# Mixture-of-experts phase: 28 light experts in place of 24, 25 units in place of 26

## What is computed

```python
scores = sigmoid(xf @ w_router)            # (264, 64)
...                                        # 4 of 8 groups, then the best 8 experts of them
gate = ...                                 # (264, 64), 0 for experts not chosen
h = silu(einsum('td,edf->tef', xb, w_gate)) * einsum('td,edf->tef', xb, w_up)
h = h * gb[..., None]
routed = einsum('tef,efd->td', h, w_down)  # 64 experts of 1024x256, 1024x256, 256x1024
shared = (silu(xf @ ws_gate) * (xf @ ws_up)) @ ws_down
```

## Time and profile before

| what | us |
|---|---|
| three runs, median (lowest to highest) | 1022.73 (1020.9 to 1023.9) |
| the profiled execution, its own time | 1022.15 |
| its span, first to last instruction | 1020.3 |
| mean granted TensorE clock | 0.974 |
| TensorE matmuls busy | 936.3 |
| VectorE, ScalarE, GpSimd busy | 504.5, 232.9, 244.0 |

### The profile page before, as it was taken

The page is one execution under the profiler, slowest core; times in us unless marked ns, Lnnn a source line. Parts: engine busy times, 40 slices in busy tenths (PEclk is TensorE's granted clock), DMA queues, the critical chain, the costliest instruction groups (busy, mean ns, idle before and its releaser), DMA issues.

```text
span 1020.3 us, 19336 instructions
## 1 busy us (share of the span) xinstructions
PE 936.3 (92%) x7882; PEld 555.5 (54%) x7882; DVE 504.5 (49%) x1040; ACT 232.9 (23%) x483; POOL 244.0 (24%) x281
## 2 busy tenths in 40 slices
PE   5999999999999998689999999999899799799795
PEld 4878877887787777536744334434333233233231
DVE  2148857885886596885523233333233223232234
ACT  3241134113411341344011111211111121111113
POOL 0039805950793099000100000000000000000000
PEclk9999999999999999979999999999899899899898
DMA  8643134114312407149589999999999999999961
GB/s 241 184 124 95 43 115 149 54 43 142 120 55 84 138 4 288 26 181 418 189 351 385 399 420 420 419 420 419 417 419 419 419 401 420 420 409 418 422 254 45
DMA packets 76742, 265.04 MB, mean 260 GB/s; under 512 B 12943, under 2 KB 44241, under 8 KB 51800
## 3 DMA queue, kind: packets, MB, share of 16 engines
q1 hardware_dynamic: 72791, 254.09, 64.4%
q0 software_dynamic: 3856, 9.64, 2.5%
HBM read 263.75 MB, written 5.89 MB: 264 GB/s over the span
## 4 chain that ended last, share of the span: by engine, by line
PE 67%; DMA 20%; DVE 6%; ACT 3%; SPq 2%; issue 2%; DVEq 0%; ACTq 0%
PE bank L1350 64%; DMA big<-in_w_up 17%; ACT big L1647 2%; SPq L401 2%; DMA big<-in_w_down 2%; DMA big<-in_w_in 1%; PE bank L629 1%; DVE big L1937 1%; PE bank L691 1%; ACT L1647 1%; DVE big L1994 1%; DVE big L1990 0%; PE bank L657 0%; DVE big L913 0%; DVE big L1185 0%
## 5 line engine op out<-in xcount | busy, mean ns | idle before, releaser
L1350 PE MATMUL bank<-big 64*64 64x64 f32 (+8 forms) x7412 | 878.6, 372 | 63.2 <-DMA big<-in_w_up 27.2
L1350 PEld LDWEIGHTS bank<-big 64*64 64x64 f32 (+4 forms) x7412 | 499.8, 143 | 401.7 <-issue 297.6
L1647 ACT ACTIVATE big<-bank 128x512 f32<-128x512 f32 (+8 forms) x283 | 121.9, 459 | 625.2 <-PE bank L1350 347.8
L1191 POOL DMA_INDIRECT big<-xg,big x26 | 26.3, 1010 | 501.2 <-PE bank L629 395.5
L2136 POOL TENSOR_SCALAR big<-big 128x256 f32<-128x256 f32 x120 | 127.3, 1062 | 0.4
L2148 POOL TENSOR_TENSOR big<-big 128x256 f32<-128x256 f32 x120 | 87.7, 730 | 0.3
L1099 DVE TENSOR_TENSOR big<-big,bank 128x512 f32<-128x512 f32 x104 | 71.5, 688 | 31.7 <-PE bank L1350 31.6
L1937 DVE SCALAR_TENSOR_TENSOR big<-big 128x256 f32<-128x256 f32 x120 | 74.4, 620 | 4.1
L1096 DVE TENSOR_TENSOR big<-big,bank 104x256 f32<-104x256 f32 x26 | 11.0, 422 | 118.9 <-issue 76.3
L1647 ACT ACTIVATE big<-big 128x272 f32<-128x272 f32 (+9 forms) x108 | 49.9, 505 | 42.3 <-DVE big L1872 11.3
L1061 DVE TENSOR_TENSOR big<-big,bank 128x256 f32<-128x256 f32 x26 | 11.0, 422 | 96.9 <-ACT big L1647 96.9
(11 more groups left out here) (156 smaller groups left out, 361.1 us busy)
## 6 DMA issues: line engine op xcount, KB each, us to landing
big<-in_w_gate SPq DMA_DIRECT2D x64, 1024.0 KB, 13.9
big<-in_w_up SPq DMA_DIRECT2D x64, 1024.0 KB, 17.3
big<-in_w_down SPq DMA_DIRECT2D x64, 1024.0 KB, 23.6
big<-in_w_in SPq DMA_DIRECT2D x29, 1024.0 KB, 5.4
big<-in_w_out SPq DMA_DIRECT2D x2, 2048.0 KB, 11.5
big<-in_state_wkv SPq DMA_DIRECT2D x32, 64.0 KB, 2.2
out_wkv_s<-big SPq DMA_DIRECT2D x32, 64.0 KB, 3.9
big<-in_x_prompt SPq DMA_DIRECT2D x2, 512.0 KB, 3.7
```

What stands on the lines that cost most here:

```text
L1191: pool.indirect_dma_start(out=x[0:n, :], out_offset=None, in_=xg, in_offset=bass.IndirectOffsetOnAxis(ap=idxu[0:n, col:col + 1], axis=0), ...
L1350: return nc.tensor.matmul(out_, lhsT=lhsT, rhs=rhs, start=start, stop=stop)
L1647: return nc.scalar.activation(out_, in_, f, **kw)
```

## The change

28 experts are light in place of 24. Fourteen triples and eleven pairs make 25 units; before there were twelve triples and fourteen pairs. Before, the order was PPP T and eleven times TP. Now it is PPP, six times TTP, and twice TP. With an odd number of units the last unit's output buffer is the other one (`ye[0]`, which is the third row of `x2p`), so the scratch row of the last Square and the buffer of the overflow pass move too.

```diff
-NSTATIC, NLIGHT = 6, 24
-UNITS = 'PPP' + 'T' + 'TP' * 11
+NSTATIC, NLIGHT = 6, 28
+UNITS = 'PPP' + 'TTP' * 6 + 'TP' * 2
...
-        xe1, ye1, oh1 = xe[0], ye[0], OH[0][:, :, 0:SLOTS]
+        xe1, ye1, oh1 = xe[0], ye[NU_E % 2], OH[0][:, :, 0:SLOTS]
...
-                link(fn(x2p[0:r, t, :], xrow[0:r, t, :], ACT.Square, accum_out=stat[0:r, t:t + 1]), 'act_chain')
+                link(fn(x2p[0:r, t % 2, :], xrow[0:r, t, :], ACT.Square, accum_out=stat[0:r, t:t + 1]), 'act_chain')
```

## The result

| what | before | after |
|---|---|---|
| median (lowest to highest), us | 1023.2 (1020.9 to 1023.9) | 1034.53 (1033.04 to 1035.69) |
| the profiled execution, its own time | 1022.15 | 1033.04 |
| its span | 1020.3 | 1031.2 |
| mean granted TensorE clock | 0.974 | 0.968 |

The ratio of after to before is 1.0105, with an interval of 1.0081 to 1.0128: slower by 11.3 us on the medians, 10.9 on the two profiled executions. The forecast was 6.2 us slower, 1028.4, with 1034.0 as the top of its range.

What follows compares the result with a forecast made beforehand. DMA bytes bound the edited stretch. Five idles +9.6, one gather -1.3 and the tail -2.1 make +6.2 on 1022.15, so 1028.4 us; range 1020.5 to 1034, chance of slower 0.64.

Steps and rivals of the forecast that it cites:

- The bound: In the stretch the change edits, weight bytes through the full DMA queue set the time: 39.9 us per triple and pair.
- The unit that is gone, at nothing: One unit of 26 removed, 17.6 us of TensorE work, gains nothing because the weight stream covers it.
- The rival in which it gives 17.6: TensorE as bound, the missing unit giving 17.6: 1004.6 us; chance 0.13 together with a weaker form, which holds nearly all.
- The gather, -1.3: One fewer gather call of token rows in the DMA queue, a gain of at most 1.3 us.
- The place and the mechanism: At five new triples behind triples, TensorE waits 5 to 9 us for up loads and the DMA queue then empties.
- e19: Expert, numbered in processing order; last of three in the first new triple behind a triple, up load landing at 632.5.
- The tail, -2.1: At the end, the last triple waits less than 1 us and its block takes a warm 7.9 us, gaining 2.1.
- The idle, 5 x 1.9 = 9.6: DMA queue idle behind five new triples that follow a triple, 1.9 us each, +9.6 in sum.
- 2.3 for the restart: A gate load into an empty queue takes 4.8 us to land, 2.3 more than its 2.49 of transfer.
- The waits for down loads: Near the end, TensorE waits 2.3 us for one down load, counted within the tail.
- upper bound of 2.9 per idle: Most that each queue idle was to cost: 5.3 us to land in place of 4.8, and 14.9 to the release.
- the u4 junction: The one triple behind a triple in the kernel before; its 0.9 us idle was taken as the lower bound.

Runs made afterwards that it cites:

- Run 2: Changed kernel, with combine(q-2) ahead of the first half of gate_up in each triple behind a triple: 1022.24 us, ratio 0.9989 to the kernel before.
- run 6: Changed kernel; combine, turn_hidden and down ahead of gate_up in triples from the seventh unit on, SyncE's down loads issued before its release wait: 1020.82 us, ratio 0.9979.
- run 7: Kernel before; combine, turn_hidden and down ahead of gate_up in triples from the seventh unit on, SyncE's down loads issued before its release wait: 1019.85 us, ratio 0.9968.
- run 11: Changed kernel, with only combine(q-2) ahead of gate_up's first half in triples from the seventh unit on and in the last pair: 1029.27 us, ratio 1.0054.

## Why the prediction was wrong, step by step

**The bound: right.** Bytes set the time from 585 us to the last triple. Runs 2, 6 and 7 differ in units, order and TensorE's waits, keep the queue full (DMA share 1.00 to 1.01), and lie within 3 us of each other.

**The unit that is gone, at nothing: right.** 15 us of TensorE work left the kernel and the time did not follow; runs 6 and 7 differ by 1 us, the kernel with fewer units being the slower. The rival in which it gives 17.6 falls.

**The gather, -1.3: right as a price.** Where nothing else is in the way, the landings of single loads across a gather are 1.25 us further apart in both traces, and after has one call fewer in the stretch. That this call gives its price back follows from the count; no run shows it by itself.

**The place and the mechanism: right.** u7 released its slots at 647.29 (647 forecast), the next gate load landed 4.8 later, at 652.1 (652 forecast). TensorE waits at u7, u10, u13, u16 and u19 4.0, 6.8, 7.2, 9.4 and 5.5 us, 32.8 in all where 5 to 9 each and some 30 were forecast. The wait of u7 is shorter than its forecast of 5.8 because u6 had waited 4.09 us for a down load (1.57 before) and released its slots at 622.40, 2.3 us later than before with the same instructions; e19's up load still landed at 632.57, before at 632.45. The share of the DMA engines falls below 1 at each of the five. The first blocks, 50 matmuls, ran at a clock of 0.72 to 0.85 (0.75 forecast); that of u7, then that of u23 behind its wait of 1.20:

```profile
632.70:642.90 10.20, 10.20 (x50) 3.34 (x51) 2.49 (x4) 0.00 (x0) 0.00 (x0) 0.77 1.02 425
...
975.16:983.06 7.90, 7.90 (x50) 3.00 (x51) 2.49 (x4) 0.00 (x0) 0.00 (x0) 1.00 1.02 424
```

**The tail, -2.1: right.** u23 waited 1.20 us, 0.2 more than the bound that was forecast, and its block took 7.90. From u23's start to the end of the span are 56.04 us, 58.10 before: -2.06.

**The idle, 5 x 1.9 = 9.6: the step that failed.** The mechanism was there at all five places, but each cost 2.5 us and not 1.9, 12.5 in all. This is 2.9 of the 4.6 us by which the profiled execution of after, 1033.04, lies above the forecast. Another 1.7 of queue time has no cause shown (below), and the median lies 1.5 over the profiled execution. The idle is in two pieces, and only the first was in my sum. The first is the time until the gate load of the release is in. From the landing of the second triple's up load to the release are 14.7, 13.9, 13.8, 14.7 and 15.3 us, 14.5 in the mean as forecast; with 2.3 for the restart and the 14.94 of queued loads off, the idles are 2.1, 1.3, 1.2, 2.1 and 2.7, together 9.3. So by my own measure the number was right. The Trainium skill, "DMA: Bandwidth & Descriptors", section "Anatomy of one DMA — SWDGE (gpsimd) path", gives some 2.0 us of fixed cost for a DMA of the GpSimd path. The trace has, for loads issued by SyncE, 2.3 to 2.4 over the 2.49 us of a full queue at the four restarts whose landing is on record, and the measurement decides.

The second piece is what comes after the first landing. I took the stream to be back in step as soon as the gate load is in. The up load lands behind it not 2.49 but 3.0, 3.7, 3.0 and 4.6 us later at the four places where both landings are on record. Counted from the last landing on record before each empty queue to the next gather, the landings lie 2.0, 1.7, 1.6, 3.6 and 3.6 us further apart than 2.485 a load and the usual 1.25 of the gather that starts there: 12.5 in all, 3.2 more than the 9.3 of the first piece. The first loads after an empty queue and that gather come together; which of the two slows the other, no run separated. Run 2 shows that it belongs to the empty queue: with the queue full, the gathers at the same places cost 1.25. A single place scatters, though. At u4, where the instructions are the same in both kernels, the same count gives 0.4 in before (583.25 to 602.25, seven loads) and 1.5 in after (580.23 to 602.82, eight loads). So the sum of five is firmer than any one of them.

The total can be read from the last triple's up load. The chain of after from 880 us:

```profile
887.42 10.12 DMA big<-in_w_up
...
917.33 17.40 DMA big<-in_w_down
...
955.38 19.64 DMA big<-in_w_up
```

It lands at 955.38 + 19.64 = 975.02, where before it was at 962.07: 12.95 later with one gather fewer, so 14.2 us of queue are lost. 12.5 of them are the junctions; the other 1.7 have no cause shown. The same count from e19's up load to this one, 124 loads in both kernels, leaves 15.6 us in after and 1.5 in before. Of what after has outside the junctions, 1.0 and 1.4 us stand beside the gathers at 672 and 802. With the tail, 12.5 + 1.7 - 1.25 - 2.06 = 10.9, the difference of the two spans; the 1.7 is the remainder, so this sum is no check of the 12.5.

**What was left out.** The waits for down loads, 18.3 us where before had 1.6, were priced only in the tail (2.3 forecast, 3.59 found). They look like a candidate for the missing us. Run 2 acquits them: it has 34.5 of them, and no loss.

**The range.** Its upper bound of 2.9 per idle would have held this, with no gain in the tail, at 1035.4. That would have been luck: the gain in the tail did come, and with it the bound is 1033.3. I cut the range at 1034.0; the profiled execution is inside and the median is 0.5 above. The bounds were drawn for the idle up to the first landing, and the refill had none. The row of the u4 junction told the time of one load, not when the stream was back in step; and there the count up to the next gather, 0.4, is even below the 0.9 of the first landing, so before gave no warning.

## What to carry to other kernels

When a stream of bytes sets the time, read each release from the queue's side. Compare how many us of work are still in the queue when the consumer's last load lands with how long the consumer then takes to free the next slot. In these runs a wait of TensorE cost nothing while the queue was full, and it was the place to put work that stood between a landing and a release. The same move cost its gaps as soon as TensorE set the pace (run 11). And price an empty queue until several loads are in at their usual distance, not until the first is in.

## What the runs showed of the hardware

- A load of 1 MB into an empty queue was in after 4.8 to 4.9 us, 2.3 to 2.4 more than its 2.49 of a full queue. The next landed 3.0 to 4.6 us behind it in place of 2.49, where a gather of 128 rows ran beside it.
- The clock of the first block behind a wait did not follow the length of the wait: 0.77 after 4.00 us, 0.83 after 6.79, 0.85 after 7.16, 0.77 after 9.36, 0.72 after 5.45. Run 2's junction had a wait of 0.62 after a combine, and its 32 matmuls took 3.64 us, as warm ones do.
- An eviction that stands alone between two groups of matmuls, two ScalarE instructions of 1.09 us together, left TensorE idle for 1.34 to 1.36 us (run 11).
- One gather of 128 rows cost the full queue 1.25 us.
